# A first phase of separate blocks becomes one stream of 92 weight strips

## What is computed

```python
hn = rmsnorm(x, ln1_g) * (1.0 + sc1) + sh1
z = hn @ w_in                                  # 1024 -> 2832 columns
(qa, ka, va, lra, ra, gb, xb, qc, kc, vc, bd, cd, xd) = split_cols(z)
# A: gated linear attention, chunks of 64 tokens, state 4 x 32 x 64
log_alpha = log_sigmoid(lra @ gla_wa2 + gla_ba) / 16
o_a = head_rmsnorm(gla_chunked(s, qa * 32**-0.5, ka, va, log_alpha)) * silu(ra)
# B: RG-LRU
xcv = causal_dwconv(xb, 4 taps) + b            # 64x64 blocks of gates on xcv
r, i = sigmoid(xcv @ rg_wa + rg_ba), sigmoid(xcv @ rg_wx + rg_bx)
log_a = -8 * r * softplus(-rg_lambda)
hs = linear_scan(exp(log_a), sqrt(-expm1(2 * log_a)) * (i * xcv), h)
o_b = head_rmsnorm(hs * gelu(gb))
# C: stick-breaking attention over qc, kc, vc and a cache of 512 past rows
# D: o_d = head_rmsnorm(bd * causal_dwconv(cd * xd, 3 taps))
```

## Time and profile before

| what | value |
|---|---|
| median of 3 runs | 3226.63 us (3226.51 to 3226.89) |
| profiled execution | 3220.0 us, its span 3218.1 us |
| mean granted TensorE clock | 0.926 |
| PE, DVE, ACT, POOL busy | 2893.8, 1443.7, 1233.0, 422.0 us |
| first phase (after setup, to the first load of the tail) | 117.9 to 1027.7 us |

### The profile page before, as it was taken

The page is one execution under the profiler, slowest core; times in us unless marked ns, Lnnn a source line. Parts: engine busy times, 40 slices in busy tenths (PEclk is TensorE's granted clock), DMA queues, the critical chain, the costliest instruction groups (busy, mean ns, idle before and its releaser), DMA issues.

```text
span 3218.1 us, 37294 instructions
## 1 busy us (share of the span) xinstructions
PE 2893.8 (90%) x14501; PEld 2325.1 (72%) x14501; DVE 1443.7 (45%) x2195; ACT 1233.0 (38%) x1745; POOL 422.0 (13%) x247
## 2 busy tenths in 40 slices
PE   3798997989976689999998999988999998799997
PEld 1375675757766467887776788776777878799997
DVE  4505134061511356666545544444454542554444
ACT  4435344362422443333344433343443333332222
POOL 0132332323300130000022000012100002200001
PEclk9799898998955689999998999998999999899998
DMA  7333242332344235555544555543655455354552
GB/s 264 131 105 98 86 131 72 111 106 83 95 122 123 87 128 181 164 170 154 180 143 138 170 185 170 159 152 91 198 171 186 153 182 157 113 180 158 164 164 76
DMA packets 404354, 458.52 MB, mean 142 GB/s; under 512 B 19067, under 2 KB 311846, under 8 KB 404198
## 3 DMA queue, kind: packets, MB, share of 16 engines
q1 hardware_dynamic: 385366, 425.96, 42.2%
q10 hardware_dynamic: 18832, 30.41, 2.6%
HBM read 385.53 MB, written 70.79 MB: 142 GB/s over the span
## 4 chain that ended last, share of the span: by engine, by line
PE 58%; DVE 5%; ACT 2%; DMA 1%; issue 1%; POOL 1%; SPq 0%; POOLq 0%; DVEq 0%; ACTq 0%
PE t_dn L1983 10%; PE t_dn L1987 9%; PE t_dn L1984 9%; PE t_dn L2023 7%; PE t_dn L2025 7%; PE t_dn L2024 7%; PE t_ob L1921 3%; PE t_sc L1898 2%; PE t_wt L1910 2%; DVE t_left L1776 1%; PE t_sc L1902 1%; DMA out_dram<-t_yrow 1%; DVE t_st L1843 1%; DVE t_st L1840 1%; DMA t_st<-o_scratch 1%
## 5 line engine op out<-in xcount | busy, mean ns | idle before, releaser
L1819 DVE SCALAR_TENSOR_TENSOR t_xs<-t_dn,modT,t_xs 128x512 f32<-128x512 f32 (+3 forms) x816 | 448.2, 580 | 335.1 <-PE t_dn L2025 199.7
L1983 PE MATMUL t_dn<-t_h_hi,t_w1h 128*128 128x512 f32 (+1 forms) x1600 | 587.5, 367 | 4.2 <-ACT t_h_hi L1701 3.5
L1987 PE MATMUL t_dn<-t_h_lo,t_w1h 128*128 128x512 f32 (+1 forms) x1600 | 567.2, 355 | 1.6 <-POOL t_h_lo L1543 1.5
L1984 PE MATMUL t_dn<-t_h_hi,t_w1l 128*128 128x512 f32 (+1 forms) x1600 | 565.0, 353 | 0.0
L2023 PE MATMUL t_dn<-t_g_hi,t_w2h 128*128 128x512 f32 (+1 forms) x1280 | 479.8, 375 | 55.2 <-DVE t_xs L1819 42.4
L2025 PE MATMUL t_dn<-t_g_lo,t_w2h 128*128 128x512 f32 (+1 forms) x1280 | 457.9, 358 | 0.0
L2024 PE MATMUL t_dn<-t_g_hi,t_w2l 128*128 128x512 f32 (+1 forms) x1280 | 456.8, 357 | 0.0
L1853 DVE TENSOR_TENSOR t_rt<-t_rt 128x512 f32<-128x512 f32 (+1 forms) x160 | 95.8, 599 | 579.4 <-ACT t_g_hi L1714 579.3
L1983 PEld LDWEIGHTS t_dn<-t_h_hi,t_w1h 128*128 128x128 f32 x1600 | 302.4, 189 | 58.0 <-issue 21.3
L1987 PEld LDWEIGHTS t_dn<-t_h_lo,t_w1h 128*128 128x128 f32 x1600 | 301.2, 188 | 45.4 <-POOL t_h_lo L1543 5.3
L1984 PEld LDWEIGHTS t_dn<-t_h_hi,t_w1l 128*128 128x128 f32 x1600 | 302.4, 189 | 31.3 <-issue 0.8
(11 more groups left out here) (241 smaller groups left out, 3689.3 us busy)
## 6 DMA issues: line engine op xcount, KB each, us to landing
t_raw<-in_mlp_w_dram SPq DMA_DIRECT2D x256, 512.0 KB, 4.6
t_w1l<-lo_scratch SPq DMA_DIRECT2D x120, 512.0 KB, 3.5
wraw<-in_w_in_dram SPq DMA_DIRECT2D x96, 512.0 KB, 3.8
t_w2l<-lo_scratch SPq DMA_DIRECT2D x96, 512.0 KB, 5.9
lo_scratch<-t_w1l SPq DMA_DIRECT2D x40, 512.0 KB, 5.4
t_raw<-in_w_out_dram SPq DMA_DIRECT2D x32, 512.0 KB, 4.9
lo_scratch<-t_w2l SPq DMA_DIRECT2D x32, 512.0 KB, 5.4
wada<-in_w_ada_dram ACTq DMA_DIRECT2D x6, 2048.0 KB, 9.6
```

The lines of the kernel that those rows point to most:

```text
L1819: ins = dve.scalar_tensor_tensor(out=cols, in0=dn[u % 4][:, s - a:t - a], scalar=modT[:, mod + f, m:m + 1], in1=cols, op0=ALU.mult, op1=AL ...
L1983: pe.matmul(out, hi[:, k, :], h_hi[:, k, a:e], start=(i == 0), stop=False)
L1984: pe.matmul(out, lo[:, k, :], h_hi[:, k, a:e], start=False, stop=False)
L1987: ins = pe.matmul(out, hi[:, k, :], h_lo[:, k, a:e], start=False, stop=(i == KT - 1))
```

## The change

`mixer_phase` becomes `front_phase`. Time is cut into **slots**. Each block has 23: slot 0 is the low-rank input, slots 1 to 22 the strips, in the new order ka, xb, gb, qa, va, ra, cd, xd, bd, kc, vc, qc. The four blocks follow each other without a break: 92 slots and 3 to run out.

- A `Flow` is a block's chain, or the sample's. Each step of a chain hangs at a fixed offset from the flow's first slot. The sample's flow begins at slot 6 of block 0.
- Block 0 is 576 columns wide: 512 prompt tokens and the 64 sample tokens. Its strips are done in two groups of 288 columns, so 48 matmuls instead of 24. There is no sample body.
- Tokens of the next block are prepared inside the current one: raw transposes at slots 4, 7, 8, 9 (copies by ACT and DVE in turn), squares in slots 4 and 5, scaled rows in 10 and 11, normalised transposes at 13, 14, 15, 17 (copies by DVE).
- The sum of squares is taken on token rows: ACT `Square` with `accum_out` over 1024 columns (L635 on), 1/rms on 128x4 values, rows scaled on DVE before they are transposed. The product with ones is gone.
- The low-rank weights are packed as hi and lo side by side (32 columns): 16 matmuls instead of 24.
- `w_lo` moves from POOL to DVE (L870), and so do all `hn_lo` (L877). POOL has nothing left here.
- PSUM: four banks `zr` in a ring for strips and chain products (before: two), two for transposes, two for updates.
- The head norms no longer stand together: B at slot 10, A at 19, D at 21. ACT loads a table 15 times in a block of the middle.

The core of the diff:

```diff
-def mixer_phase(nc, const, mixc, x_prompt, x_sample, ...
+def front_phase(nc, const, mixc, x_prompt, x_sample, ...
+    WIDE, HALF = BLK + DEC, (BLK + DEC) // 2
+    SLOTS = len(STRIPS_IN) + 1
+    LAG = 6
...
+    flows = [Flow(0, 0, False, 0), Flow(1, 0, True, LAG)] + [Flow(b + 1, b, False, b * SLOTS) for b in range(1, NBLK)]
+    N_SLOTS = NBLK * SLOTS + 3
...
+    RING_JOBS = [("y", 2, 1), ("g0", 5, 2), ("g1", 6, 2), ("nB", 10, 2), ("o", 17, 2), ("nA", 19, 2), ("nD", 21, 2)]
+    RAW, XN, PAST_AT = (4, 7, 8, 9), (13, 14, 15, 17), SLOTS + 11
...
+        found += [("kd", f.e, 0, "act") for f in at(slot, 6)]
+        found += [("va", f.e, j, "act") for f in at(slot, 10) for j in range(1 if f.sample else 2)]
```

ScalarE's queue in a slot (`ring_out` copies out what the chain and the strip of the slot before made):

```diff
+            def weights_hi(slot):
...
+                act.wait_ge(w_in_sem[n % 2], 16 * (n // 2 + 1))
+                if n >= 2:
+                    act.wait_ge(z_full, ring_no["z", old, len(groups(old // SLOTS)) - 1] + 1)
+                act.activation(w_hi[n % 2][:, :, :], wraw[n % 2][:, :, :], ACT.Copy).then_inc(w_hi_ok, 1)
...
+            def step(slot):
...
+                if b is not None:
+                    tokens_hi(b)
+                if has_weights(slot + 1):
+                    weights_hi(slot + 1)
+                if slot:
+                    ring_out(slot - 1)
+                    for job in tp_jobs(slot - 1):
+                        turned(job)
...
+                        square_rows(b, 2 * i)
+                        square_rows(b, 2 * i + 1)
...
+                for f in at(slot, 4):
+                    decays(f)
+                for f in at(slot, 8):
+                    roots(f)
```

VectorE's queue in a slot:

```diff
+            def step(slot):
...
+                if has_weights(slot + 1):
+                    weights_lo(slot + 1)
+                for job in tp_jobs(slot - 1) if slot else []:
+                    turned(job)
...
+                for f in at(slot, 4):
+                    decayed_keys(f)
+                    conv_b(f)
+                for f in at(slot, 7):
+                    rg_input(f)
+                for f in at(slot, 8):
+                    rg_scan(f)
```

TensorE's transposes (`turn(job)`) and its queue in a slot:

```diff
+            def turn(job):
+                kind, e, j, by = job
+                u, bank = tp_no[kind, e, j], tp_bank(kind, e, j)
+                if u >= 2:
+                    by, n = tp_freed[u - 2]
+                    pe.wait_ge(tp_free[by], n)
...
+            for slot in range(N_SLOTS):
+                for f in at(slot, 2):
+                    low_rank(f)
+                for j in range(2):
+                    for f in at(slot, 5 + j):
+                        gate(f, j)
...
+                for job in tp_jobs(slot):
+                    turn(job)
...
+                if slot < NBLK * SLOTS:
+                    strip(slot)
```

More of the change, by code:

```diff
@@ L384, in mixer_phase @@
[L384 to L393, removed]
@@ new lines, in strip_out @@
+            def strip_out(slot):
+                b, i = divmod(slot, SLOTS)
+                before(b, i)
+                rows = 2 * RANK if i == 0 else P
+                for g, (a, e) in enumerate(groups(b)):
+                    bank = full("z", slot, g)
+                    ins = act.activation(target(i, 0)[:, a:min(e, BLK)], bank[0:rows, 0:min(e, BLK) - a], ACT.Copy,
+                                         scale=scale_of(i))
+                    if e > BLK:
+                        ins = act.activation(target(i, 1)[:, 0:DEC], bank[0:rows, BLK - a:e - a], ACT.Copy, scale=scale_of(i))
+                    ins.then_inc(z_free, 1)
@@ L788, in _ @@
+            act.preload_act_table_set(EXP_LN)
+            for i in range(TPB + 1):
+                square_rows(0, i)
+            inverse_rows(0)
+            for job in OPEN:
+                turned(job)
+            for slot in range(N_SLOTS):
+                step(slot)
         @block.vector
@@ new lines, in weights_lo, with tokens_lo @@
+            def weights_lo(slot):
+                n = weight_no(slot)
+                dve.wait_ge(w_hi_ok, n + 1)
+                dve.tensor_tensor(w_lo[n % 2][:, :, :], wraw[n % 2][:, :, :], w_hi[n % 2][:, :, :].bitcast(F32),
+                                  ALU.subtract).then_inc(w_lo_ok, 1)
+            def tokens_lo(b):
+                n = WIDE if b == 0 else BLK
+                for k in range(KT):
+                    dve.wait_ge(hi_ok, KT * b + k + 1)
+                    dve.tensor_tensor(hn_lo[:, k, 0:n], hT[:, k, 0:n], hn_hi[:, k, 0:n].bitcast(F32),
+                                      ALU.subtract).then_inc(lo_ok, 1)
@@ L905, in body, with conv_d @@
+            def conv_d(f):
+                n, cx = f.n, cxp[f.m]
+                dve.wait_ge(z_free, ring_no["z", f.b * SLOTS + 14, len(groups(f.b)) - 1] + 1)
+                if f.e == 0:
+                    dve.wait_ge(x_stored, 16 * (KT + 1))
+                elif not f.sample:
+                    dve.wait_ge(o_stored["D"][0], 16 * f.b)
+                chain.link(dve.tensor_tensor(cx[:, :, 2:2 + n], cd[f.m][:, :, 0:n], cx[:, :, 2:2 + n], ALU.mult))
                 for j in range(2):
-                    y = oT[:, 6 + j, 0:n]
@@ new lines, in norm, with update @@
+            def norm(f, kind):
+                pe.wait_ge(nsq_ready, norm_no[kind, f.e] + 1)
+                for j in range(2):
+                    bank = bank_for("n" + kind, f.e, j)
+                    pe.matmul(bank[:, 0:f.n], head_ones[:, :], nsq[:, j, 0:f.n], start=True, stop=True).then_inc(z_full, 1)
+            def update(f, c):
+                u, r0 = us_no[f.e, c], CHUNK * (c % 2)
+                wait(pe, us_used, u - 1)
+                if c == 0:
+                    last = ("va", f.e, 0 if f.sample else 1)
+                    pe.wait_ge(tp_free["act"], tp_freed[tp_no[last]][1])
+                pe.matmul(us[u % 2][:, 0:GW], kdt[f.m][r0:r0 + CHUNK, c // 2, :], vt[f.m][r0:r0 + CHUNK, c // 2, :],
+                          start=True, stop=True).then_inc(us_full, 1)
```

1223 lines of the change are left out of this document (641 added, 582 removed).

## The result

| | before | changed |
|---|---|---|
| median | 3226.63 us | **3244.76 us** (3242.31 to 3246.66, 3 runs) |
| ratio | | 1.0055, 95% interval 1.0033 to 1.0078 |
| span of the profiled execution | 3218.1 us | 3244.8 us |
| first phase, to the tail's first load | 1027.7 us | 1050.1 us |
| mean granted TensorE clock | 0.926 | 0.930 |

The change makes the kernel slower by half a per cent. I had forecast 3202 us. Of the 26.7 us between the two profiled spans, 22.4 lie ahead of the tail's first load (0.9 of them in the setup) and 4.3 in the tail, whose code is the same. In the first phase alone PE was busy for 800.8 us and idle for 109.0; now it is busy for 745.5 and idle for 185.8. So the change took 55 us of PE's time away and gave 77 us of waits back.

The account below looks back on a forecast made before the run. It took PE with its waits as the limit. Opening, four blocks and end summed to 997.8 us against 1027.7 (-29.9), plus 5 for signals: -25 from the 3226.6 median, 3202 us; 8-in-10 range 3110 to 3256.

Parts of the forecast that it names:

- block 0: First block, with the sample: 170.7 us of PE work, 57.9 of waits and 6.8 for the clock, 235.4 in all.
- block 3 with the end: Last block, no tokens to prepare and shorter waits, 180.6 us; last copies and stores 7.6 us.
- slot-by-slot waits: PE's waits in a steady block, from queued ACT and DVE operations: 44.0 us together, longest 8.5 at slot 7.
- The table load's price: On ACT, 1.28 us a load with the next operation directly behind; loads go from 7 to 15 a block.
- DVE's 0.75: Convolution steps on DVE take 0.75 us each away from POOL, against 1.445 beside it.
- the walk: Adding up ACT's and DVE's queued operations in each slot from the end of PE's previous strip, giving PE's waits.
- the term for the clock: PE's loss at 1.2 GHz behind five places with long waits: 6.3 us a steady block, 6.8 in block 0.
- my work: PE's work per block without waits: 170.7 us in block 0, 152.8 in blocks 1 and 2, 145.8 in block 3.
- rival 2: Twelve waiting places a block, not five, each leave a stretch at 1.2 GHz: 3256 us, slower; 23% chance.
- Its signs: Rival 2 would show a phase clock below 0.8 and strips over 6 us in slots 8 to 10 and 13 to 16.
- Rival 3: On ACT, each table switch also costs a drain of 1.38 us, 44 us in all: 3246 us, slower; 3% chance.
- The claim on `w_lo`: Moving `w_lo` from POOL to DVE costs nothing for POOL; DVE gets 1.22 us a slot, counted among the waits.

Follow-up runs that it names:

- first filled kernel: Changed kernel with dummy matmuls put into TensorE's waits before gates and transposes, 448 more matmuls: 3207.98 us, 0.9939 of the kernel before.
- the state updates first: Changed kernel with transpose copies first on ScalarE and VectorE, a joint Ln/Exp table, and VectorE's state updates ahead of `w_lo`: 3108.96 us, 0.9629 of the kernel before.

## Why the prediction was wrong

Point by point, first-strip to first-strip:

| term | predicted | measured |
|---|---|---|
| opening, to strip 1 | 160.5 | 159.6 |
| block 0 | 235.4 | 267.9 |
| block 1 | 210.6 | 224.5 |
| block 2 | 203.1 | 210.5 |
| block 3 with the end (180.6 + 7.6) | 188.2 | 187.6 |
| signals of some 50 waits | 5 | in the above |
| sum | 1002.8 | 1050.1 |

**What was right.** The opening, and most of the slot-by-slot waits: 8.49, 8.32 and 8.31 us at slot 7 (8.5); 5.88 at slot 5 of block 2 (6.2); 2.35 at slot 6 (2.4); 2.12 at slot 12 (2.2); 3.26 at slots 14 and 15 (3.9 with the update); 3.87 at slot 21 (3.7). The waits of block 0 were 57.9 in the sum and 59.2 in the trace. The table load's price and DVE's 0.75 held.

**What was right by luck.** In sum the walk had 208 us of waits and clock, of which some 24 for the clock, so 184 of waits. PE's idle time is 169.6, and 5.9 of that lie behind the last strip, so I had the waits 20 us too long (slots 8 and 9 at 2.2 each instead of 2.7, slots 13 to 15 at 8.7 instead of 10.5, slot 0 at about 1.8 instead of 4.1). That hid a part of the error below. In block 3 two errors cancel: its work was 145.8 in the sum, and PE is busy for 159.6; its waits, clock and end were 42.4, and PE is idle for 28.0. That its time came out within 1 us says nothing for the sum.

**The step that failed** is the term for the clock: "For the five places with long waits (slots 1, 5, 7, 14 with 15, 21) I take 6.3 us", and 6.8 in block 0, together some 24 us. PE's busy time in the four blocks is 208.7 + 180.4 + 172.2 + 159.6 = 720.9, while my work was 170.7 + 2 x 152.8 + 145.8 = 622.1, with the 24 us for the clock 646: 75 us short. Filling the waits returned some 46 us of the kernel's time. A clock of 0.85 in block 0 means that 0.3 of 267.9 us = 80 us were at 1.2 GHz; in all four blocks it is 201 us, waits included. Two errors lie in the term. I counted long waits only: five places a block, where by the records 31 of the 88 strips took over 0.4 us more than an undisturbed one (6.6 us in block 0, 5.8 in the others), eleven of them in block 0. There the waits at slots 5, 6, 7, 8, 9, 11, 12 and 13 to 17 follow each other with one strip or less between. And I priced a place at some 1.3 us, from a row of three norm pairs that lost 1.9 behind a single wait of 3.06 us. The strips alone lost some 44 us, about 1.4 in each of those 31, up to 2.7; the products and transposes next to them lost too, as the gate products of 3.78 instead of 1.98 us show.

That is rival 2, to which I gave 23%, at a price of 3256 us (measured 3244.8). Its signs came only in part: strips of 6.5 to 7.9 us stand in slots 8, 9 and 14 of blocks 1 and 2, but the clock of the phase is 0.88 and not below 0.8. Rival 3's 3246 lies still nearer to the measured time, by chance: no load has the gap that it needs. The evidence for rival 2 stood in the earlier trace rows: the sample's body at 0.50 with PE busy four fifths of the time. Against it I had set blocks with waits of up to 6.1 us at 0.90. That was no argument, since those blocks lose by this clock too: 0.91 over 194.9 us in the earlier trace rows means 35 us at 1.2 GHz, a loss of up to 17 us, and I put 6.3 on a block with twice the waits.

**A smaller part** remains. The first filled kernel is busy for 776.1 us in the four blocks; less 448 fills at 0.235 that is 671, still 49 over my 622. Its clock of 0.92 in block 0 and 0.98 to 0.99 behind explains about 30 (half of the low share of each length). The last 20 can be work that I left out: the sample's own products in block 0, the cache's transposes in block 1, or strips somewhat over 5.6. I have not separated these, so their cause stays open. The tail, whose code is the same, took from 2186 to 2195 us in these runs and 2190.4 before. Its 4.3 us lie at its start: in its first 100 us the clock is 0.56, before 0.65, and its first `head_ones` product comes 91.8 us behind the first load instead of 83.2; part of that is made up later. Why the clock is lower there stays open.

**The claim on `w_lo`** ("I cost at nothing for POOL ... DVE gets 1.22 a slot, which is in the walk"): the price was in the walk, but I drew nothing from the place that it takes in DVE's queue. It is the one part of the change that was undone alone, and it costs 24 us.

## What to carry to other kernels

When waits are scattered between matmuls, price each twice: its own length, and the slowed work behind it; in the one pair of runs that shows both, a microsecond of removed wait brought 1.9. Check the term against the kernel that you have: its granted clock already says what such work loses. And a filled wait is a cheap experiment that tells the clock's part from the queue's. In an engine's queue, put what PE waits for next (bank copies, state updates) ahead of what it needs a strip later (the next weight half); this order, with 14 table loads fewer, was worth 154 us of 3245. A pair of banks that two engines free in turn is only as early as the later one, so such moves have to be tried together (25 and 17 us alone, 60 together).

## What the runs showed of the hardware

The share of idle time alone doesn't give the granted clock. The block of the earlier trace rows had 20.1 us of idle time in 194.9 and a clock of 0.91; block 1 with the state updates first had 18.8 in 184.0, the same tenth, and 0.95. And of the two strips of slot 13 with the same waits just before them one had 0.66 and the other 1.00. With dummy matmuls in the waits the clock stood at 0.98 to 0.99 although ACT and DVE were no faster. GpSimd's subtraction beside DVE stretched a 0.752 us step to 1.081 on average. The Trainium skill, GPSIMD Engine Reference, section Specifications, says that GpSimd shares its SBUF interfaces with VectorE, and that there is contention with VectorE's instructions that take two SBUF inputs. The convolution's step is one of these, and its two rows agree.
